# Seven matrix operands of a hybrid S5, mLSTM and attention kernel, placed 32 bytes further along in SBUF

## What is computed

```python
def conv_gated_mlp(xn, w_up, conv_w, conv_b, w_down):
    gate, val = jnp.split(xn @ w_up, 2, axis=-1)
    return (jax.nn.silu(causal_dwconv(gate, conv_w, conv_b)) * val) @ w_down
```

## Time and profile before

| | |
|---|---|
| median of three runs | 1041.33 us (1042.63, 1041.33, 1036.88) |
| the profiled execution, its own time | 1042.44 us |
| its span, first to last instruction | 1040.9 us |
| TensorE matmul busy | 1024.1 us, 98% |
| TensorE weight load busy | 898.0 us, 86% |
| DVE, ACT, POOL busy | 705.5, 540.5, 490.7 us |
| mean granted TensorE clock | 0.998 |

### The profile page before, as it was taken

How to read it: one execution, slowest core, us unless ns; L and a number is a source line. 1 busy time by engine, 2 the same in 40 slices (tenths; PEclk the granted TensorE clock), 3 DMA queues, 4 the chain that set the end, 5 groups by cost and what they waited for, 6 DMA issues and landing times.

```text
span 1040.9 us, 18153 instructions
## 1 busy us (share of the span) xinstructions
PE 1024.1 (98%) x6848; PEld 898.0 (86%) x6848; DVE 705.5 (68%) x1020; ACT 540.5 (52%) x939; POOL 490.7 (47%) x437
## 2 busy tenths in 40 slices
PE   9999999999999999999999999999999999999997
PEld 8787778888899999988888777888899999988886
DVE  6798764499877777863334775669877777773332
ACT  6545665455565565732323566564666565742221
POOL 8998930364877877200100222243877877500000
PEclk9999999999999999999999999999999999999999
DMA  7541025231323222243224111232323323133222
GB/s 237 169 119 58 15 94 182 81 122 54 144 86 121 99 104 81 81 142 122 101 101 152 62 43 61 83 120 82 118 86 122 110 92 121 60 117 127 102 81 81
DMA packets 31293, 107.47 MB, mean 103 GB/s; under 512 B 7232, under 2 KB 9536, under 8 KB 26368
## 3 DMA queue, kind: packets, MB, share of 16 engines
q1 hardware_dynamic: 31232, 106.69, 30.0%
HBM read 102.09 MB, written 3.15 MB: 101 GB/s over the span
## 4 chain that ended last, share of the span: by engine, by line
PE 84%; DVE 10%; issue 2%; ACT 2%; SPq 1%; DMA 1%; POOL 0%; DVEq 0%; ACTq 0%
PE bank L2050 16%; PE bank L2051 15%; PE bank L2052 15%; PE bank L2358 11%; PE bank L2357 11%; PE bank L2359 11%; PE bank L2074 2%; DVE wlo L1376 2%; DVE alo L1728 2%; DVE t_lo L1728 1%; PE bank L2497 1%; PE bank L2474 1%; DMA raw<-wstream 1%; PE bank L2197 1%; PE bank L2262 1%
## 5 line engine op out<-in xcount | busy, mean ns | idle before, releaser
L1376 DVE TENSOR_TENSOR wlo<-raw,whi 128x1024 fp32r<-128x1024 f32 x105 | 147.3, 1407 | 103.1 <-ACT whi L876 102.9
L876 ACT ACTIVATE whi<-raw 128x1024 fp32r<-128x1024 f32 x105 | 110.6, 1055 | 139.1 <-PE bank L2052 87.4
L2357 PE MATMUL bank<-t_hi,shi 128*128 128x256 f32 x576 | 162.1, 281 | 5.1 <-DVE t_lo L1728 5.1
L2358 PE MATMUL bank<-t_lo,shi 128*128 128x256 f32 x576 | 161.8, 281 | 0.0
L2359 PE MATMUL bank<-t_hi,slo 128*128 128x256 f32 x576 | 161.8, 281 | 0.0
L2050 PE MATMUL bank<-xhi,whi 128*128 128x512 f32 x384 | 152.0, 396 | 0.8 <-DVE wlo L1376 0.8
L2051 PE MATMUL bank<-xlo,whi 128*128 128x512 f32 x384 | 149.6, 390 | 0.0
L2052 PE MATMUL bank<-xhi,wlo 128*128 128x512 f32 x384 | 149.6, 390 | 0.0
L2050 PE MATMUL bank<-ahi,whi 128*128 128x512 f32 (+1 forms) x374 | 141.4, 378 | 0.2
L2052 PE MATMUL bank<-ahi,wlo 128*128 128x512 f32 (+1 forms) x374 | 140.9, 377 | 0.0
L2051 PE MATMUL bank<-alo,whi 128*128 128x512 f32 (+1 forms) x374 | 140.9, 377 | 0.0
(11 more groups left out here) (309 smaller groups left out, 2245.8 us busy)
## 6 DMA issues: line engine op xcount, KB each, us to landing
raw<-wstream SPq DMA_DIRECT2D x105, 512.0 KB, 3.3
raw<-spairs SPq DMA_DIRECT2D x36, 1024.0 KB, 4.8
xin<-xT SPq DMA_DIRECT2D x8, 256.0 KB, 6.5
raw<-wstream SPq DMA_DIRECT2D x8, 256.0 KB, 5.8
h<-xT SPq DMA_DIRECT2D x1, 2048.0 KB, 8.8
u_scratch<-uperm SPq DMA_DIRECT2D x1, 1024.0 KB, 5.5
uc<-u_scratch SPq DMA_DIRECT2D x8, 128.0 KB, 4.2
bandsb<-band SPq DMA_DIRECT2D x1, 1024.0 KB, 4.8
```

The source lines that it names most:

```text
L876: A(whi[:, t % RING, :], raw[:, t % RAWS, :], ACT.Copy).then_inc(hi_done, 1)
L1376: V.tensor_tensor(wlo[:, t % RING, :], raw[:, t % RAWS, :], whi[:, t % RING, :].bitcast(f32), ALU.subtract).then_inc(lo_done, 1)
L2357: MM(dst, wh, hi[:, b, :], start=b == 0, stop=False)
L2358: MM(dst, wh, lo[:, b, :], start=False, stop=False)
```

## The change

One number, 192, becomes 224 wherever it occurs. All fourteen quarter tiles (seven high, seven low) move by 32 bytes, and with them the small tiles behind them. Their rows then begin 224 bytes past a multiple of 1024. The weights, `xhi`, `ahi`, `alo` and `ohi` stay. No instruction is added, removed or moved on any engine, and no wait, size or transfer changes.

```diff
-    past_a = base + size([P, FJ, SEQ]) + 192
+    past_a = base + size([P, FJ, SEQ]) + 224
...
-    x_quarter_at = {"b22": xn_at + 192, "t4": xn_at + 192 + 8192}
+    x_quarter_at = {"b22": xn_at + 224, "t4": xn_at + 224 + 8192}
     for k, name in enumerate(("b11", "b21", "t2", "t1", "t3")):
-        x_quarter_at[name] = base + 2 * 2048 + 192 + 8192 * k
+        x_quarter_at[name] = base + 2 * 2048 + 224 + 8192 * k
...
-    rows, u4u3 = plan(("rows", [P, 2 + 5 * QW], f32), ("u4u3", [P, 2, QW], f32), start=xn_at + 192 + 2 * 8192)
+    rows, u4u3 = plan(("rows", [P, 2 + 5 * QW], f32), ("u4u3", [P, 2, QW], f32), start=xn_at + 224 + 2 * 8192)
```

More of the change, by code:

```diff
@@ L270, in build @@
     u2, value_row, c22 = rows[:, 2 + 2 * QW:2 + 3 * QW], rows[:, 2 + 3 * QW:], rows[:, 2 + 4 * QW:]
-    assert xn_at + 192 + 2 * 8192 + size([P, 2 + 5 * QW]) + 2048 <= xn_at + 2 * size([P, KB, SEQ])
+    assert xn_at + 224 + 2 * 8192 + size([P, 2 + 5 * QW]) + 2048 <= xn_at + 2 * size([P, KB, SEQ])
     xn = at("xn", [P, KB, SEQ], alo_at + 14 * 2048)
```

## The result

| | median us | runs | range |
|---|---|---|---|
| before | 1039.54 | 11 | 1032.12 to 1045.37 |
| after | 1045.66 | 11 | 1043.34 to 1047.21 |

The ratio is 1.007, 95% interval 1.0042 to 1.0099: slower, by 0.7%. The kernel before spreads over 13 us, the changed one over 4.

A forecast was written before the change was run, and what follows sets the result against it. It took the pace of TensorE's own matmuls, busy 98% of the span, as the bound. All terms were 0, so 1042.44 + 0, or 1041.3 us in terms of the median, with a range of 1028 to 1050.

The forecast's parts named there:

- likeliest case: Whole kernel: nothing changes, the median stays at 1041.3 us, own range 1035 to 1044; chance 0.38.
- term 1: The 3024 quarter matmuls: pace unchanged, taken as 0, bounded by 12.8 us less and 6.7 us more.
- What decides between the paces: Quarter matmuls on TensorE: either how TensorE starts after a stop or where operands lie; evidence for the place called weak.
- slower rival: Whole pair stage: at 224 every weight load 192 ns, pace 120.0, 6.7 us more; chance 0.24, 0.35 with beyond 120.0.
- fingerprint: Pair loops, L2357 to L2359: matmul lengths of 276, 281 and 283 ns would follow paces of 113.3, 117.8 and 120.0.
- the loads are a little longer in the slower two: Quarter weight loads: 188 ns at pace 113.3; some or all 192 ns at paces 117.8 and 120.0.
- better-pace rival: Pair loops: at 224 113.3 ns becomes usual, 12.8 us less in both layers; chance 0.16 both, 0.11 one, together 0.27.
- Terms 2 to 4: Making the quarter operands, the small tiles on DVE, ACT and POOL, and everything else including `block3`: each 0.

The follow-up runs named there:

- again224: The changed kernel with no edit, run again beside the kernel before: 1044.96 us, ratio 1.0099.
- run 5: Not a label, part of "one run 5 us low": one of three unchanged-kernel runs, 1036.88 us, 5.1 us under the mean of the other two.
- full0: The kernel before with every 192 made 0, so the quarter operands lie at 0: 1049.88 us, ratio 1.0122.
- bare test: Code without the model's work, only matmuls of 256 columns after starts at 192 and 224: at 224 all 60 short starts settled between 117.9 and 118.7 ns.
- bare map: Paces of 256-column matmuls without the model's work, operand at 19 offsets: 120.0 ns at 0, 113.3 at 192, 118.0 to 118.8 at 224.
- small224: The kernel before with only the small tiles moved from 192 to 224, quarter operands kept at 192: 1036.9 us, ratio 1.0019.
- N: Columns of the one matmul just ahead of 36 quarter matmuls at 192, varied in code without the model's work: 113.3 or 117.8 ns depending on N.
- again192: The kernel before with no edit, run and profiled again: 1035.76 us, ratio 1.0003.
- relay: The kernel before with the start behind the 2.8 us stop released by a one-column ScalarE copy, not by VectorE: 1037.61 us, ratio 1.0008.
- fill kernels: The kernel before with 13 unread 512-column matmuls and one of 400 or 352 columns in the stop ahead of t4's product: 1030.62 and 1043.15 us.

## Why the prediction was wrong

The range (1028 to 1050) held the time. The likeliest case, no change, did not come: slower, which had 0.35, did.

- **The step that failed is term 1, "I take 0".** It compared 224 with the pace of the profile at hand, 117.8 ns, and took that for the kernel's pace. Of that profile's pace the change costs only 0.55 ns, 1.7 us, and there "no measurable change" would have been right. But the profile showed a run with both loops in the worse pace, which 11 of the 90 later runs resemble. By the times, the share of loops in the better pace over those 90 runs is (2 x 36 + 43) / 180 = 0.64. The change takes it away: 0.64 x 2 x 6.4 = 8.2 us, plus 1.7 us, 9.9 in all. Measured means differ by 9.0 us (1044.9 in again224, 1035.9 over the 90). The eleven runs of the result had worse draws: 2, 4 and 5 of them have two, one and no such loop, a share of 0.36. That makes 4.7 + 1.7 = 6.4 us, and the means there differ by 6.0 (1045.2 and 1039.2).
- **"What decides between the paces" was right in both its answers**, start and place, and wrong in the weights. The trace had 113.3 ns after two of the three starts named, at 192, and never at 0; the three run times held one run 5 us low. I read this as a spread that 224 would share ("with the starts as before"), but whether a pace can be had at all depends on the place. The prediction also overlooked a fourth start in the first trace of before, in pair 0 between the two that it names. Its first matmul, and the first and last of 21 distances behind it:

```profile
255.38 0.36 PE L2357 MATMUL bank<-t_hi,shi 128*128 128x256 f32 x1
...
255.69 0.28 PE L2359 MATMUL bank<-t_hi,slo 128*128 128x256 f32 x1
...
258.17 0.28 PE L2359 MATMUL bank<-t_hi,slo 128*128 128x256 f32 x1
```

These take 2.48 us, 118 ns each. So in layer 0 of that trace the two paces stood two to two, with the operands at 192 throughout.

- **The slower rival** had the right sign and the wrong shape: not 120.0 ns and all loads at 192 ns, but 118.3 and all at 188. The loads' length is no fingerprint of the pace: it is 188 ns at 113.3 and at 118.3, so "the loads are a little longer in the slower two" is no rule either, and that a matmul and the next load hold each other up was not shown. Its price was 6.7 us over the profile, while the true one is 1.7 over that profile and 14.4 over the best runs (2880 x 5.0 ns). The repeat by 256 bytes, which it assumed, is real. The 120.0 ns at 0 carried over as priced, in full0.
- **The better-pace rival** never came true at 224, in 60 settled starts of the bare test and in both profiles, but it describes the kernel before: by the times its loops are at 113.3 in more than half of the cases.
- **The Trainium skill's rule** (independent ports for the streamed operand and the weight load, in "TensorE: Matmul & The Clock Gate", section "Step-by-step: what each phase is for") would have given 0. The bare map contradicts what I drew from it: the same instructions run from 113.3 to 120.0 ns by nothing but the operand's place. The 109.2 ns that the prediction took from "Back-to-back issue gap" of the same page is the gap that the Trainium skill gives for a matmul by itself, without a budget for weight loads, and should not have been put to this stream. That both streams meet in SBUF is my reading; what exactly they contend for was not shown.
- **The size of the range was in part luck.** It holds 1045.66 us because it reached up to 120.0 ns, a pace that did not come, and its base of 1041.3 us was the median of three runs that by their times had five of six loops in the worse pace; 1045.66 lies outside the likeliest case's own range of 1035 to 1044.
- Terms 2 to 4 held: TensorE waited 2.5 us in each layer for the last quarter operand (2.6 and 2.5 before); moving the small tiles costs nothing (small224); `block3`'s rows stayed at 389 ns; no engine became the bound.

What stays open: why the map has these values and this period, what the moment is measured against, and which share of the draws is the start's and which the returning clock's. Computed from the starts in the first trace of before, settled matmuls of 512 columns begin at one and the same remainder to 6.67 ns over each stretch. Within a stretch that follows from their pace, 34 x 6.67 = 226.7 ns; but the remainder is also kept across the stops, and drifts by only 1.3 ns from 19 to 937 us. So there is some fixed grid of 16 cycles at 2.4 GHz; whose it is, no run tells.

## What to carry to other kernels

When the same matmul has two paces in one trace, the profile shows one draw and not the kernel: take several profiles, or the spread of the times, before pricing a change against it. Where TensorE is the bound, sweep the distance of the streamed operand from the weights in steps of 32 bytes in a bare loop, for each column count by itself, since one run gives the whole map. And an idle stop ahead of a long loop can be filled with matmuls that nobody reads, so that the loop starts at a chosen moment and the clock stays up; the width that does it must be measured. Here the width found in the bare test carried over to the full kernel; whether it outlives a change of the code ahead was not tried.

## What was not expected of the hardware

- The pace of matmuls of 256 columns depends on where the operand lies modulo 256 bytes: 113.3 ns at 192, 118.3 at 224, 120.0 at 0. For 512 columns it is 226.7 at 0 and up to 234.6 elsewhere. So the 32 bytes from 192 to 224 are 4.4% of the pace.
- At one place several steady paces exist (113.3 and 117.8 ns at 192). Which one TensorE falls into repeats with the matmul ahead of the stream (both starts agree at 50 of 50 values of N), and it keeps it for 170 us while all other engines work. A stretch at half clock can change it: from 113 to 117.8 ns in again192, from 118 to 113 in relay.
- After a stop of 2.6 us the granted clock fell to 1.2 GHz for 3.4 us in some runs and not in others (again192, not the first profile of before); with the stop filled by matmuls, the mean clock was 0.998 or 0.999 in all 22 runs of the two fill kernels, against 0.994 to 0.999 in the runs of before beside them.
